# First layer of the compression in three fp32r passes over pairs of batches, beside the former fp32 passes over four

## The reference, cut to what matters

```python
def compress(rows, params):
    w1, b1, w2, b2 = params
    B, T, G, dh = rows.shape
    n_cmp = (T - CMP_BLOCK) // CMP_STRIDE + 1
    idx = jnp.arange(n_cmp)[:, None] * CMP_STRIDE + jnp.arange(CMP_BLOCK)[None, :]
    blocks = rows[:, idx].transpose(0, 1, 3, 2, 4).reshape(B, n_cmp, G, CMP_BLOCK * dh)
    return jax.nn.gelu(blocks @ w1 + b1) @ w2 + b2
```

## Time and profile before

| | before |
|---|---|
| median of 3 runs | 626.97 us (624.81 to 627.13) |
| the profiled execution: its time, its span | 627.12 us, 625.4 us |
| TensorE busy | 589.9 us (94%) |
| VectorE, ScalarE, GpSimd busy | 310.3, 230.6, 76.5 us |
| mean granted TensorE clock | 0.991 |

### The profile page before, as it was taken

The page is one execution under the profiler, slowest core; times in us unless marked ns, Lnnn a source line. Parts: engine busy times, 40 slices in busy tenths (PEclk is TensorE's granted clock), DMA queues, the critical chain, the costliest instruction groups (busy, mean ns, idle before and its releaser), DMA issues.

```text
span 625.4 us, 12374 instructions
## 1 busy us (share of the span) xinstructions
PE 589.9 (94%) x5118; PEld 515.0 (82%) x5118; DVE 310.3 (50%) x785; ACT 230.6 (37%) x529; POOL 76.5 (12%) x127
## 2 busy tenths in 40 slices
PE   7899998999899999998999999999999999998993
PEld 5899997887888887997898887666567899997992
DVE  5722224051675223463474656767654447762265
ACT  5543345140323113332332544445353342222333
POOL 0017432020201115404200000000000000000000
PEclk9999998999999999999999999999999999998998
DMA  9347722643612316933722120201111433306104
GB/s 301 140 122 234 263 70 81 254 124 103 204 63 82 105 35 201 309 96 110 262 69 69 48 60 30 68 2 34 35 35 35 124 89 89 114 2 237 35 2 143
DMA packets 45673, 69.99 MB, mean 112 GB/s; under 512 B 4145, under 2 KB 36081, under 8 KB 45362
## 3 DMA queue, kind: packets, MB, share of 16 engines
q1 hardware_dynamic: 38016, 44.84, 23.1%
q0 software_dynamic: 6880, 23.24, 11.2%
q10 hardware_dynamic: 722, 1.12, 0.5%
HBM read 65.22 MB, written 8.13 MB: 117 GB/s over the span
## 4 chain that ended last, share of the span: by engine, by line
PE 88%; DVE 6%; ACT 3%; DMA 2%; issue 1%; ACTq 0%; SPq 0%; DVEq 0%
PE m L1530 53%; PE s L1697 10%; PE s L1821 4%; PE o L1835 4%; PE t L1828 3%; PE t L1672 2%; PE t L1723 2%; DMA U<-in_x_p 2%; PE m L1611 2%; DVE U L1274 1%; PE s L1737 1%; PE o L1782 1%; PE t L1661 1%; ACT U L903 1%; PE o L1808 1%
## 5 line engine op out<-in xcount | busy, mean ns | idle before, releaser
L1530 PE MATMUL m<-h_hi,w_hi 128*128 128x272 f32 x448 | 133.1, 297 | 0.0
L1530 PE MATMUL m<-h_hi,w_lo 128*128 128x272 f32 x448 | 129.2, 288 | 0.0
L1530 PE MATMUL m<-h_lo,w_hi 128*128 128x272 f32 x448 | 128.7, 287 | 0.0
L1530 PE MATMUL m<-w_hi,h_hi 128*128 128x256 f32 (+2 forms) x360 | 104.9, 291 | 3.6 <-DVE U L1478 2.0
L1530 PE MATMUL m<-w_lo,h_hi 128*128 128x256 f32 (+2 forms) x360 | 102.5, 285 | 0.0
L1530 PE MATMUL m<-w_hi,h_lo 128*128 128x256 f32 (+2 forms) x360 | 102.4, 284 | 0.0
L1530 PEld LDWEIGHTS m<-h_hi,w_hi 128*128 128x128 f32 x448 | 84.2, 188 | 10.0 <-issue 7.3
L1164 DVE TENSOR_TENSOR w_lo<-raw,w_hi 128x1024 fp32r<-128x1024 f32 (+2 forms) x62 | 71.2, 1156 | 37.4 <-ACT w_hi L916 37.3
L1530 PEld LDWEIGHTS m<-h_hi,w_lo 128*128 128x128 f32 x448 | 84.5, 189 | 0.0
L1530 PEld LDWEIGHTS m<-h_lo,w_hi 128*128 128x128 f32 x448 | 84.5, 189 | 0.0
L1530 PEld LDWEIGHTS m<-w_hi,h_hi 128*128 128x128 f32 (+1 forms) x360 | 68.4, 190 | 5.5 <-DVE U L1478 2.3
(11 more groups left out here) (278 smaller groups left out, 885.8 us busy)
## 6 DMA issues: line engine op xcount, KB each, us to landing
raw<-in_w_in SPq DMA_DIRECT2D x36, 512.0 KB, 4.0
U<-in_x_p SPq DMA_DIRECT2D x8, 512.0 KB, 7.1
raw<-in_w_o SPq DMA_DIRECT2D x8, 512.0 KB, 4.1
raw<-in_w_in SPq DMA_DIRECT2D x8, 256.0 KB, 3.8
U<-in_ck_win POOLq DMA_DIRECT2D x8, 256.0 KB, 3.4
U<-in_cv_win POOLq DMA_DIRECT2D x8, 256.0 KB, 5.9
raw<-in_w_pa SPq DMA_DIRECT2D x8, 256.0 KB, 4.1
raw<-in_w_pb SPq DMA_DIRECT2D x4, 512.0 KB, 3.4
```

Of the source, the lines that this page charges most:

```text
L1530: ins = mm(out, lhs(a, k), rhs(b, k), start=(k == 0 and a + b == 0), stop=(k == n - 1 and a == 1))
```

## The change

It works in ten chunks (`NCH`): the prompt first, then four pairs of batches, for keys and then for values. A pair's first layer is done in three passes of fp32r with 252 columns each: `hidh` has hi x hi and weight-lo x hi (32 matmuls), `hidl` weight-hi x lo (16). The weights are split once for keys and once for values (`w1hi` on ScalarE, `w1lo` on VectorE, in place of the raw weights). Each of a pair's four tiles is now cast by ScalarE to `xt_hi` and then subtracted by VectorE to `xt_lo`, and VectorE's subtraction is what frees the PSUM bank. Of the last tile ScalarE casts one half and VectorE the other. The main group of a pair is made in two halves (`half`), one on either side of tile 2. `hidl` of a pair stands behind the first two tiles of the next pair. The destination is laid out so that 252 columns in a row belong together: batch, head and block are interleaved, and so an element of a tile is written 16 bytes from the one before. The prompt chunks stay in fp32, 16 matmuls with 62 columns. ZA now comes ahead of U in `SLOTS`. Further small edits: `sq` of the sample rows is one step earlier, `split` of C0 one group earlier, the prompt's rows are loaded first.

```diff
@@ -47,8 +47,8 @@
 
 SLOTS = [("B0", "tm", C_KCMP, 256), ("B1", "tm", C_KSEL, 256), ("C0", "tm", C_KWIN, 280),
          ("A0", "tm", C_Q, 256), ("A1", "tm", C_Q + 256, 256), ("V0", "tm", C_V, 256), ("V1", "tm", C_V + 256, 256),
+         ("ZA0", "tr", C_ZA, 256), ("ZA1", "tr", C_ZA, 256),
          ("U0", "tr", C_U, 256), ("U1", "tr", C_U + 256, 256),
-         ("ZA0", "tr", C_ZA, 256), ("ZA1", "tr", C_ZA, 256),
          ("ZB0", "tr", C_ZB, 256), ("ZB1", "tr", C_ZB + 256, 256)] + \
         [(f"RA{n}", "tr", C_R + 256 * n, 256) for n in range(4)] + \
         [(f"RB{n}", "tr", C_R + D + 256 * n, 256) for n in range(4)] + \
...
-    for c in range(6):
-        for n in range(8 if c % 3 < 2 else 1):
-            order += [("xt", c, n)]
-            if n % 2:
-                if c == 4 and n == 3:
-                    order += [("sp", i) for i in range(NT + 1)]
-                main(BETWEEN_ROWS[c][n // 2])
-            if c and n == (1 if c % 3 < 2 else 0):
-                order += [("kc", c - 1)]
-        if c == 3:
-            order += [("ln2", i) for i in range(NT + 1)]
-        if c == 5:
-            main(BEFORE_LAST_HIDDEN)
-        order += [("hid", c)]
+    order += [("w1hi", 0)]
+    for c in range(NCH):
+        behind = [("hidl", c - 1)] if c - 1 in PAIRS else []
+        if c % 5 == 0:
+            order += [("xt", c, 0)] + behind
+            main(IN_PROMPT_CHUNK)
+            if c:
+                order += [("w1hi", 1), ("w1lo", 1), ("kc", c - 1)]
+            order += [("hid", c)]
+            if c == 0:
+                order += [("w1lo", 0)]
+            continue
+        order += [("xt", c, 0), ("xt", c, 1)] + behind + [("half",) + groups[state["n"]][1:], ("xt", c, 2)]
+        main(1)
+        n = order.index(groups[state["n"] - 1]) + 1
+        after = order[n:]
+        del order[n:]
+        order += [("xt", c, 3), ("kc", c - 1), ("hidh", c)] + after
+        order += {6: [("ln2", i) for i in range(3)], 7: [("ln2", i) for i in range(3, NT + 1)],
+                  8: [("sp", i) for i in range(3)], 9: [("sp", i) for i in range(3, NT + 1)]}.get(c, [])
+    order += [("hidl", NCH - 1)]
     main(AFTER_LAST_HIDDEN)
-    order += [("kc", 5)]
...
+                elif kind == "w1hi":
+                    act.wait_ge(w1_loaded[s[1]], 16)
+                    if s[1]:
+                    for k in range(2):
+                        ins = nc.scalar.copy(w1_hi[k][:, :, :], w1_at[s[1]][:, 8 * k:8 * k + 8, :])
+                    ins.then_inc(w1_hi_done, 1)
...
+                elif kind == "xt" and s[1] in PAIRS:
+                    c, n = s[1], s[2]
+                    b, r = divmod(n, 2)
+                    act.wait_ge(t_done, t + 1)
+                    if c > 1:
+                        act.wait_ge(hid_half, PAIRS.index(c))
+                    for g in range(G - n // 3):
+                        ins = nc.scalar.copy(turned(xt_hi, r, g, b), TB[t % 2][64 * g:64 * g + 64, :].rearrange("p (q o n) -> p q o n", q=4, o=2))
+                    ins.then_inc(xt_hi_done, 1)
...
+                elif kind == "w1lo":
+                    dve.wait_ge(w1_hi_done, s[1] + 1)
+                    dve.wait_ge(hid_sum, 5 if s[1] else 1)
+                    for k in range(2):
+                        ins = v.tensor_tensor(w1_lo[:, 8 * k:8 * k + 8, :], w1_at[s[1]][:, 8 * k:8 * k + 8, :], w1_hi[k][:, :, :].bitcast(F32), ALU.subtract)
+                    ins.then_inc(w1_lo_done, 1)
...
+                    if c == 1:
...
+                    else:
+                        dve.wait_ge(hid_sum, c - (c == 6))
+                    if n == 3:
+                        if c > 1:
+                            dve.wait_ge(hid_half, PAIRS.index(c))
+                        v.tensor_copy(turned(xt_hi, r, 1, b), tb[64:128, :].rearrange("p (q o n) -> p q o n", q=4, o=2)).then_inc(xt_hi_dve, 1)
+                    dve.wait_ge(xt_hi_done, 4 * PAIRS.index(c) + n + 1)
+                    for g in range(G):
+                        if n == 3 and g == 1:
+                            dve.wait_ge(xt_hi_dve, PAIRS.index(c) + 1)
+                        ins = v.tensor_tensor(turned(xt_lo, r, g, b), tb[64 * g:64 * g + 64, :].rearrange("p (q o n) -> p q o n", q=4, o=2),
+                                              turned(xt_hi, r, g, b).bitcast(F32), ALU.subtract)
                     ins.then_inc(t_dve, 1)
...
+                    if kind == "half":
+                        continue
...
+                elif kind in ("hidh", "hidl"):
...
+                    first = kind == "hidh"
+                    if first:
+                        pe.wait_ge(w1_hi_done, c // 5 + 1)
+                        pe.wait_ge(w1_lo_done, c // 5 + 1)
+                        pe.wait_ge(xt_hi_done, 4 * PAIRS.index(c) + 4)
+                        pe.wait_ge(xt_hi_dve, PAIRS.index(c) + 1)
+                        if c >= 2:
+                            pe.wait_ge(hid_ready, c - 1)
+                    else:
+                        for n in range(4):
+                            wait_evacuated(pe, T_AT[("xt", c, n)])
+                    for j in range(16):
+                        o, q = divmod(j, 4)
+                        at = 512 * q + 256 * (o % 2) + 4 * (o // 2)
+                        end = at + 4 * NCS
+                        w = w1_hi[j // 8][:, j % 8, :]
+                        if first:
+                            mm(out[:, 0:end - at], w, xt_hi[:, at:end], start=(j == 0), stop=False, skip_group_check=True)
+                            ins = mm(out[:, 0:end - at], w1_lo[:, j, :], xt_hi[:, at:end], start=False, stop=False, skip_group_check=True)
+                        else:
+                            ins = mm(out[:, 0:end - at], w, xt_lo[:, at:end], start=False, stop=(j == 15), skip_group_check=True)
+                    ins.then_inc(hid_half if first else hid_sum, 1)
```

More of the change, by code:

```diff
@@ L143 @@
                    ("b1k", 1), ("b1v", 1), ("b2k", 1), ("b2kr", 1), ("b2v", P)])
-BETWEEN_ROWS = {0: (0, 1, 0, 1), 1: (0, 1, 0, 1), 3: (0, 1, 0, 1), 4: (0, 1, 1, 1)}
-BEFORE_LAST_HIDDEN, AFTER_LAST_HIDDEN = 1, 1
+NCH = 10
+PAIRS = [c for c in range(NCH) if c % 5]
+IN_PROMPT_CHUNK, AFTER_LAST_HIDDEN = 1, 1
 AFTER_KEYS = (1, 1, 2)
@@ L223, in plan @@
     order += [("hT", 3)]
-    main(4)
+    main(3)
     order += [("split", 2, 0)]
     main(1)
-    order += [("low", 2, 0), ("split", 2, 1)]
-    main(1)
-    order += [("low", 2, 1)]
+    order += [("low", 2, 0), ("split", 2, 1), ("low", 2, 1)]
+    main(2)
     order += [("out_cmp",), ("wsT",), ("rope", 0)]
@@ L349 @@
 MAIN_AT = {s: n for n, s in enumerate(MAIN)}
+HALVED = [("main",) + s[1:] for s in ORDER if s[0] == "half"]
 def freed_by(s):
@@ L387 @@
 RING = 3
-LOADS = [(w, b) for w in ("kc", "vc") for b in list(range(NB)) + ["p"]]
+LOADS = [(w, b) for w in ("kc", "vc") for b in ["p"] + list(range(NB))]
 LOAD_AT = {x: n for n, x in enumerate(LOADS)}
@@ L843, in _ @@
                     store(pv_cmp, sv_cmp, kq[:, 0:NT, 384:512], kq[0:TS, NT, 384:512], cmp_out)
-                    pool.wait_ge(rows_ready, 3)
-                    load_upto(RING)
+                    pool.wait_ge(rows_ready, 4)
+                    for n in range(1, RING):
+                        load(n)
                 elif s[0] == "rope":
@@ L851, in _ @@
                         if s[1] == 0:
+                            load(0)
+                            loaded[0] = RING
                             store(pk_sel, sk_sel, kq[:, 0:NT, c0:c0 + 128], kq[0:TS, NT, c0:c0 + 128], out_done)
@@ L1022, in _ @@
                     else:
                         act.wait_ge(rope_step, ROPE_STEPS[3])
[L1024 to L1030 removed]
+                    act.wait_ge(hid_sum, c + 1)
@@ L1522, in _, with passes @@
             mm = nc.tensor.matmul
-            def passes(out, lhs, rhs, n, before=None):
-                for k in range(n):
+            def passes(out, lhs, rhs, n, before=None, ks=None):
+                for k in ks or range(n):
                     if before:
@@ L1538, in _ @@
                     wait_t_bank(pe, t)
-                if kind == "warm":
-                    pe.wait_ge(pads_zero, 1)
-                    zeros = q_bd[:, 0:4, :].rearrange("p b n -> p (b n)")
-                    for _ in range(WARM):
-                        mm(O[:, 0:P], zeros, zeros, start=True, stop=True)
+                if kind == "spread":
                     pe.wait_ge(st_ready, 2)
@@ L1593, in _ @@
                     ins.then_inc(t_done, 1)
-                elif kind == "main":
-                    n = MAIN_AT[s]
-                    wait_main_bank(pe, n)
+                elif kind in ("main", "half"):
+                    n = MAIN_AT[("main",) + s[1:]]
+                    if s not in HALVED:
+                        wait_main_bank(pe, n)
                     out = M[n % 2]
@@ L1617, in _ @@
                         continue
-                    if MAIN_AT[s]:
+                    if n and s not in HALVED:
                         pe.wait_ge(lo_done, 2 * sl + 2)
```

(9 more changed lines are left out.)

232 lines of the change are left out of this document (117 added, 115 removed).

## The result

The changed kernel takes **667.7 us** (median of 4 runs, 663.92 to 670.94); the kernel before takes 627.05 us beside it (4 runs, 624.81 to 628.78). The ratio is 1.065, with a 95% interval of 1.058 to 1.072. The prediction was 624.7 us with a range up to 633: wrong in sign and out of the range.

A forecast was written before the change was run, and what follows sets the result against it. It took TensorE to bound the kernel, with hand-offs over two t banks as second limit in the compression. Compression -4.5 us and softmax +2.1 gave -2.4 on 627.12, so 624.7 us, range 617.5 to 633.

The forecast's parts named there:

- the price of a piece: In each pair's tiles: a ScalarE cast piece takes 0.58 us and a VectorE piece 0.69 us.
- slow pieces: Rival, compression: pieces written every 16 bytes cost x more, stretch grows 56x; 653 us at 0.5 us more; chance 0.10.
- the fall to 1.2 GHz in each pair: Rival: TensorE's clock falls ahead of `hidh`, up to 1.5 us a pair, 12 in all, 637 us; chance 0.08.
- the forecast's own case: Whole kernel: 624.7 us predicted, likeliest case 622 to 626.5 us, chance 0.40.
- A pair's row of hand-offs: In each pair: tiles, casts and subtractions delay the first `hidh` product to 8.38 us; a pair takes 12.15 us.
- waits eat all 12.9 us: Rival, compression: hand-offs cost 0.3 us more per pair, time stays at 627 us (626.5 to 630); chance 0.14.
- From the start to the first `hidh`: Start of the compression: the first pair's `hidh` ends 18.2 us behind the start, `hidh` itself taking 3.76.
- From pair 4's `hidh` to pair 6's: Value side's start: 23.8 us from pair 4's end to pair 6's, with a 3.65 us wait, plus 0.7 for the clock.
- The work: Compression: TensorE's own work falls by 12.9 us, as 58.0 us of first layers give way to 45.1.
- The softmax: Softmax of the first four batches: four added table loads of 1.28 us each delay the first product, +2.1 us.
- The other edits taken at nothing: Remaining edits move steps within other engines' waits: taken as 0, between -0.5 and +0.5 us.
- If two subtractions overlap: Part of the shorter-waits rival: each pair loses 0.25 us of waiting, 2.0 in all; that rival's chance 0.28.

The follow-up runs named there:

- e3: The changed kernel with 24 filler matmuls of 252 columns in TensorE's wait ahead of each `hidh`, their sums overwritten; 655.1 us.
- e2: The changed kernel with every piece written contiguously, 64 columns in a run, and the shift by one block left out; 629.4 us.
- e1: The changed kernel with pieces written in steps of 8 bytes, not 16, and matmuls reading 254 columns in one run; 633.0 us, ratio 1.012.
- e8: e1 with tanh in place of gelu as the function of the U groups alone, so values differ; 631.3 us.
- e5: e1 with VectorE casting its half of a pair's last tile ahead of its subtraction of tile 2; 629.6 us, ratio 1.003.

## Why the prediction was wrong

**The step that failed is the price of a piece.** The sum for a pair took "ScalarE's pieces 0.58 and VectorE's 0.69 us", the rows of contiguous copies, for writes in steps of 16 bytes. They take 1.067 and 1.077. The term was in the text as a rival: "If a piece that writes every 16 bytes costs x more, the stretch grows by 8 x 7x = 56x". With x = 0.42 as the mean over the seven that gives 23 us; e3 and e2 measured 2.80 a pair, 22 for eight. I gave it 0.10, on the ground that a small reduction read PSUM at such a stride for nothing. That row was of another memory and another side of the instruction, and I put it above a rule that spoke of this one: by the Trainium skill (SBUF — State Buffer, Door 1: The DMA port swizzle) each access to a new line pays, and it did.

**The second part is the clock, and the two rivals were one.** I held slow pieces (to 653) and the fall to 1.2 GHz in each pair (8 x 1.5 = 12) for separate cases. The clock falls in the waits that the slow pieces make: 0.50 for 3.1 us behind one of them, and half clock behind all eight. With the waits filled (e3) or short (e1, e2) no `hidh` runs at half clock. e3 gives back 1.5 us a pair. 653 and 12 make 665, and the profiled run has 666.7. That they meet so closely is in part luck: 653 has x = 0.5 where 0.42 was measured, some 5 us too much, and leaves out the 4.1 us of hand-offs below.

**What held, and by how much.** e2 is the forecast's own case, with contiguous pieces, and took 629.4 us, within the range. Against the terms of the sum:

- A pair's row of hand-offs: 8.38 us to `hidh`, measured 8.82 (131.43, less `hidh`'s 3.81, to 140.25); a pair 12.63 for 12.15, and from pair 6's `hidh` to pair 8's 13.08 each for 12.55 (177.68, 190.76, 203.84). The hand-overs take longer than I had put them: the first product starts 0.26 us behind the end of VectorE's cast (139.30 + 0.69, 140.25). Over the stretch this and the tail make 131.8 for 127.65, 4.1 us. With the right layout the rival "waits eat all 12.9 us" would have come nearest.
- From the start to the first `hidh`: 18.2 - 3.76 = 14.4, measured 14.9. From pair 4's `hidh` to pair 6's: 24.5 with the clock's 0.7, measured 24.8 at 0.93.
- The work: 12.9 us less; TensorE's busy time in the stretch is 124.75 before and 113.66 in e2, 11.1 less.
- The softmax: +2.1, measured +1.6, and e8 shows that it is the loads. An activation again starts 0.01 us behind its load (311.50 + 1.28, 312.79), so no drain shows here either. The figures for load and drain that the prediction takes from the Trainium skill stand on its page ScalarE: Activation LUTs, under What ACT_TABLE_LOAD costs.
- The other edits taken at nothing: they don't stand apart from the runs' own variation of some 2 us ahead of the stretch.
- "If two subtractions overlap": they don't (2.20 for two of 1.08).

So with the measured price of a piece, the clock's rival and the hand-offs as measured, the same sum gives -4.5 + 2.1 + 4.1 + 22 + 12 = 36 us, for 39.6 measured in the span. Of the remaining 3.9, 1.8 are ahead of the stretch; the rest is where I have no run that separates it: the clock of 0.73 up to the first `hidh`, which was 0.71, 0.89 and 1.00 in runs of e1, e5 and e2.
